# State-space stage: the step-size chain ahead of a weight split, the dense transposes in the other PSUM ring, the norm by token tile; projection units of 512 by 512

## Chip, cores and metric

The kernel runs on one core of one Trainium2 chip. The metric is device time in microseconds of one execution; three runs are given as their median. Profiled times are those of one further execution.

## What is computed

Three transformer-like blocks run one after the other on x of 1024 tokens by 1024 channels, float32. Block 1 mixes gated linear attention with a spatial gating unit and ends in an MLP. Block 2 mixes a two-way state-space scan with differential attention. Block 3 mixes a convolution branch with a gated recurrence. Each mixer ends in an output projection that is added to the residual. The part of block 2 around the change:

```
z, xbc, dt_f, dt_b, q, k, v, g = split(h @ w_in)
xbc = silu(depthwise_conv5(xbc) + b)          # 1536 channels: x, B, C
dt  = softplus(dt + dt_bias)                  # 16 heads, two directions
a_cs = cumsum(dt * A, within 128-token chunks)
y = ssd_chunked(x, dt, A, B, C), forward and backward, + D * x
y_ssm = rms_norm(y * silu(z)) per group of 512, * ssm_norm_g
mix = concat(y_ssm, y_attn) @ w_out;  h = layer_norm(ALPHA * h + mix)
```

Blocks 1 and 3 project likewise: x + concat(a, b) @ w_out, the inner dimension being 1024 in block 1 and 2048 in blocks 2 and 3, there in two parts of 1024.

## The kernel before

Every large product is made in three passes of rounded float32 (fp32r): both operands are split into a high and a low part, and high x high, high x low and low x high are summed in PSUM. `three` lists the pairs, `mms` issues them (the matmul is L211). Activations lie transposed in `HTh` and `HTl`: 8 k-tiles of 128 channels by 1024 tokens.

*Weight units.* A weight is streamed in units of 128 x 2048 elements. `sp_unit` issues the load of unit i into ring `WR` once unit i-3 has been used; `act_unit` makes the high part in `WH` (L320, after the landing and the use of unit i-2); `dve_unit` the low part in `WL` (L328, after the high part); `pe_unit` waits for both. A unit was 256 columns by 8 k-tiles. The engines' programs are written out by hand, each runs in its own order, and each unit call stands at a place chosen in that order.

*Projections.* `tm` fills one PSUM bank of 512 columns with two token tiles by 256 columns: 2 x 8 x 3 matmuls of 256 columns, the stationary operand being a tile of `HTh` or `HTl`. `dve_added` adds the bank to the residual X. `pe_proj` does four units; `pe_proj_led` two units and then two more in the order `LED`, in which the first tokens are finished early so that the next norm can start. The tags are 1 (output projection of block 1, input `sgu`), `o2a` and `o2b` (the two halves of block 2's), `o3b` and `o3c` (block 3's). `fm` is the other orientation: 24 matmuls of 512 columns into one bank.

*PSUM.* Two rings of four banks: `PD` and `PB`. `take` gives the next bank and waits for whoever must free the previous content.

*State-space stage.* `pe_ssm_first` makes the step sizes dt and the first halves of channel tiles 8 and 10. Then `weave` interleaves two generators on each engine by weights: `steps_` (the dt chain, weight 10) and `dense(0)` (channel tiles 8, 10, 0 and 1, weight 32). A channel tile m takes: fm(m,0) and fm(m,1) on TensorE; two copies into the one buffer `pad2` (L2399, ScalarE, after the convolution of the tile before) and the first tap (L2405); four more taps on VectorE (L2457); silu (L2414); transposes xbcT(m) on TensorE into `PB` (for tile 10 the CB products); copies out of them (L2378, L2383). The dt chain: transposes of dt (L2194), bias (L2261), Abs, Exp and Ln on ScalarE, softplus and dA (L2265 to L2270), the cumulative sums by matmul (ACS), their copy and differences and the row tables QT (L2275 to L2295), transposes of QT ("rows"), copies TT and LT (L2250, L2252), tables RR (L2303). Worked out from `weave`, the orders before are:

```
TensorE: dt transposes; fm 8,1; ACS; fm 10,1; rows; fm 0,0; xbcT 8 (two banks);
         fm 0,1; fm 1,0; CB (two); fm 1,1; xbcT 0; then fm 2,0; fm 2,1; xbcT 1; scan 0
ScalarE: unit; pad 8; tap; Abs,Exp,Aexp; Ln; silu 8; ldt; pad 10; tap; xs 8,0;
         exponentials; xs 8,1; TT,LT; silu 10; unit; pad 0; tap; CB; silu 0; pad 1 ...
VectorE: unit; dtb2; tap 8; dtsp,ldm,dA; taps 8; acs_; wd0,nn,QT; wd; taps 10 (two);
         RR; taps 10; unit; taps 0; diag; taps 1
```

After it four scans (`*_ssm_scan`, one for each quarter of the heads) are woven with the dense work of the next quarter. A scan step takes banks of `PB` for two segment matmuls and the states st, which L2644 adds and frees, and of `PD` for the Y and off products. After scans 1 and 3 `out_` normalises y: squares on ScalarE, two multiplies of 128 x 2048 (L2752), transposes, scaled copies (L2740) and stores.

## Time and profile before

| what | value |
|---|---|
| median of three runs | 3786.94 us (3786.23 to 3787.26) |
| the profiled execution | 3784.53 us, its span 3782.8 us |
| TensorE matmul busy | 3609.8 us, 95% of the span |
| weight loads of TensorE | 3036.7 us, 80% |
| VectorE, ScalarE, GpSimd busy | 2251.6 us, 1668.6 us, 468.9 us |
| mean granted TensorE clock | 0.98 of 2.4 GHz |

The state-space stage lies between about 1187 and 1600 us of the span; the projections at 360 to 455 (block 1), 2305 to 2470 (block 2) and 3462 to 3645 us (block 3). Busy shares are of the whole span; a group in brackets at the end of a row, `[9.33 <-DVE t L2270]`, is the time that the engine stood idle before it and the line that ended the wait.

### The profile page before, as it was taken

How to read it: one execution, taken by the hardware profiler on the slowest of the kernel's cores; microseconds unless marked ns; L12 is line 12 of the kernel's file. 1: busy time of each engine (PE TensorE's matmuls, PEld its weight loads, DVE VectorE, ACT ScalarE, POOL GpSimd, SP SyncE). 2: the span in 40 equal slices, each digit the busy share in tenths (PEclk: the TensorE clock that was granted, in tenths of full speed). 3: DMA queues.
4: the chain of work that ended last, by engine and by line, in shares of the span. 5: the costliest groups of instructions: out<-in, count | busy, mean ns of one | idle time of the engine just before them, and what ended most of it. 6: DMA issues, size and time to landing. Idle time of an engine off the chain costs nothing.

```text
span 3782.8 us, 48362 instructions
## 1 busy us (share of the span) xinstructions
PE 3609.8 (95%) x20222; PEld 3036.7 (80%) x20222; DVE 2251.6 (60%) x2947; ACT 1668.6 (44%) x2123; POOL 468.9 (12%) x373
## 2 busy tenths in 40 slices
PE   8999989999998999999999989999999999999998
PEld 7778968888876787877777759978777888778998
DVE  4545353456666765655656662468889888843332
ACT  4333344431114544467667772145455554442132
POOL 0001032200000121200000000012222222210001
PEclk9999999999999899999999999999999999999999
DMA  3012023342212011011111123121111111153111
GB/s 110 23 40 90 26 81 109 112 159 89 89 69 90 23 34 40 18 51 34 37 28 34 29 86 140 42 82 34 45 45 39 56 51 45 34 213 110 45 40 67
DMA packets 227389, 244.85 MB, mean 65 GB/s; under 512 B 10007, under 2 KB 190180, under 8 KB 227172
## 3 DMA queue, kind: packets, MB, share of 16 engines
q1 hardware_dynamic: 222391, 224.92, 18.4%
q10 hardware_dynamic: 4781, 16.84, 1.2%
q8 instruction: 160, 2.62, 0.3%
q14 instruction: 57, 0.47, 0.0%
HBM read 191.40 MB, written 50.33 MB: 64 GB/s over the span
## 4 chain that ended last, share of the span: by engine, by line
PE 77%; DVE 12%; ACT 5%; issue 3%; DMA 1%; POOL 0%; SPq 0%; ACTq 0%; DVEq 0%; POOLq 0%
PE pd L211 63%; PE pq L211 11%; PE pd L366 2%; DVE t L3520 2%; DVE t L328 1%; DVE t L3528 1%; PE pq L366 1%; DVE t L3965 1%; ACT t L3125 1%; ACT t L320 1%; DVE t L3952 0%; DVE t L3950 0%; DVE t L3197 0%; DVE t L2078 0%; DVE t L3215 0%
## 5 line engine op out<-in xcount | busy, mean ns | idle before, releaser
L211 PE MATMUL pd<-t 128*128 128x512 f32 (+2 forms) x15104 | 2904.1, 353 | 32.5 <-ACT t L3716 9.8
L211 PEld LDWEIGHTS pd<-t 128*128 128x128 f32 x15104 | 2407.6, 191 | 459.8 <-issue 90.9
L211 PE MATMUL pq<-t 128*128 128x128 f32 (+5 forms) x3782 | 635.7, 330 | 75.0 <-DVE t L4001 15.7
L211 PEld LDWEIGHTS pq<-t 128*128 128x128 f32 (+2 forms) x3782 | 484.3, 181 | 187.4 <-issue 44.4
L320 ACT ACTIVATE t<-t 128x2048 fp32r<-128x2048 f32 (+3 forms) x133 | 212.6, 1599 | 633.2 <-PE pd L211 590.8
L328 DVE TENSOR_TENSOR t<-t 128x2048 fp32r<-128x2048 f32 (+3 forms) x133 | 257.3, 1935 | 173.7 <-ACT t L320 173.2
L1919 DVE TENSOR_TENSOR t<-pd,t 128x512 f32<-128x512 f32 x256 | 172.9, 689 | 104.9 <-PE pd L211 102.7
L3248 DVE COPY t<-pd 128x512 f32<-128x512 f32 x64 | 44.2, 691 | 218.6 <-PE pd L366 218.6
L3528 DVE SCALAR_TENSOR_TENSOR t<-t 128x1024 f32<-128x1024 f32 x120 | 173.8, 1448 | 0.5
L3520 DVE SCALAR_TENSOR_TENSOR t<-t 128x1024 f32<-128x1024 f32 x120 | 169.1, 1409 | 2.1
L3917 POOL TENSOR_TENSOR t<-t 128x512 f32<-128x512 f32 x56 | 96.0, 1714 | 592.8 <-ACT t L3861 299.4
L2061 POOL TENSOR_TENSOR t<-t 128x2 f32<-128x2 f32 x8 | 10.4, 1306 | 1258.4 <-DVE t L3365 849.0
L3861 ACT ACTIVATE t<-t 128x1024 f32<-128x1024 f32 x56 | 59.5, 1062 | 228.8 <-DVE t L3952 228.8
L3125 ACT ACTIVATE t<-t 128x1024 f32<-128x1024 f32 x128 | 145.9, 1142 | 13.8 <-DVE t L3202 13.7
L3197 DVE CUSTOM_DVE_ANT_0 t<-pq,t 128x1024 f32<-128x1024 f32 x128 | 151.2, 1219 | 0.0
L366 PE MATMUL pd<-t 128*128 128x128 f32 x808 | 115.8, 285 | 25.0 <-ACT t L3106 5.9
L744 DVE TENSOR_TENSOR t<-pd,t 128x512 f32<-128x512 f32 x48 | 33.2, 691 | 175.9 <-PE pd L211 175.9
L366 PEld LDWEIGHTS pd<-t 128*128 128x128 f32 x808 | 97.4, 147 | 47.5 <-ACT t L3167 9.0
L3965 DVE COPY_PREDICATED t<-t,pq 128x512 f32<-128x512 int32 x128 | 94.4, 741 | 51.3 <-PE pq L211 50.7
L3131 ACT ACTIVATE t<-t 128x1024 f32<-128x1024 f32 x64 | 73.7, 1151 | 104.5 <-DVE t L3207 104.5
L3919 POOL TENSOR_TENSOR t<-t 128x512 f32<-128x512 f32 x56 | 112.2, 2003 | 0.0
L366 PE MATMUL pq<-t 128*128 128x128 f32 x516 | 73.7, 285 | 18.7 <-DVE t L624 5.1
(345 smaller groups left out, 2830.8 us busy)
## 6 DMA issues: line engine op xcount, KB each, us to landing
t<-in_w_in_dram SPq DMA_DIRECT2D x97, 512.0 KB, 4.3
t<-in_w_out_dram SPq DMA_DIRECT2D x20, 1024.0 KB, 5.4
t<-in_w_in_dram SPq DMA_DIRECT2D x16, 1024.0 KB, 5.3
t<-in_w_mlp_dram SPq DMA_DIRECT2D x64, 256.0 KB, 3.5
u_scratch<-t SPq DMA_DIRECT2D x64, 256.0 KB, 3.3
t<-in_w_mlp_dram SPq DMA_DIRECT2D x16, 1024.0 KB, 5.0
t<-u_scratch SPq DMA_DIRECT2D x15, 1024.0 KB, 7.2
t<-in_x_dram SPq DMA_DIRECT2D x16, 512.0 KB, 9.2
```

The lines of the kernel that those rows point to most:

```text
L211: ins = e.matmul(out, l, r, start=(first and j == 0), stop=(last and j == n - 1), skip_group_check=True)
L320: e.activation(WH[i % 2][:, 0:z], WR[i % 3][:, 0:z], ACT.Copy).then_inc(*at.inc("wh", "wh", i))
L328: e.tensor_tensor(WL[i % 3][:, 0:z], WR[i % 3][:, 0:z], WH[i % 2][:, 0:z].bitcast(F32), SUB).then_inc(*at.inc("wl", "wl", i))
L366: ins = e.transpose(b[:, j * 128:(j + 1) * 128], s, ident[:, :])
L1919: e.tensor_tensor(X1[:, tt, half(nh)], PD.of("down", j, tt, nh)[:, :], X1[:, tt, half(nh)], ADD).then_inc(*at.inc("dve", "xadd", j, tt, nh ...
L3125: e.activation(s[:, r, :], s[:, r, :], ACT.Exp, bias=x[:, 2 + r:3 + r], accum_out=x[:, 4 + r:5 + r]).then_inc(*at.inc("act", "sexp", n))
L3197: e.tensor_tensor_reduce(out=s[:, r, :], in0=PQt[r][:, :], in1=bias[:, 896 - 128 * tt:896 - 128 * tt + 1024], scale=2.0 ** -(h + 1), scala ...
L3520: e.scalar_tensor_tensor(a[:, :], p[:, k:k + S], taps(k, g), a[:, :], MUL, ADD).then_inc(*at.inc("dve", "ctaps", g))
L3528: e.scalar_tensor_tensor(a[:, :], p[:, k:k + S], taps(k, g), a[:, :], MUL, ADD).then_inc(*at.inc("dve", "ctaps", g))
L3917: e.tensor_tensor(v4(z[:, :], w_)[:, :, 0, :], v4(k[:, :], w_)[:, :, 0, :], v4(dd[:, :], w_)[:, :, 0, :], MUL).then_inc(*at.inc("pool", "h ...
L3919: e.tensor_tensor(v4(z[:, :], w_)[:, :, 1, :], v4(q[:, :], w_)[:, :, 1, :], v4(dd[:, :], w_)[:, :, 1, :], MUL).then_inc(*at.inc("pool", "h ...
L3965: e.copy_predicated(At[:, th * 4:th * 4 + 4, :], bc(Mi[:, l:l + 1, :], [128, 4, 128]), four(PB.of("lv", h, l, th))).then_inc(*at.inc("dve" ...
```

## The change

In the state-space stage, the dt chain on ScalarE and VectorE stands ahead of the weight split instead of being woven behind it, and its later parts are spaced anew (weight 16); the load of that split's weight is issued between the two halves of the stores before the stage; xbcT and CB take banks of `PD` instead of `PB`; the norm multiplies by token tile. In the projections, twelve units are 512 columns by 4 k-tiles (`pe_quarter`, one bank for each token tile, two units adding to the same columns); the `LED` units and unit 0 and 1 of `o2a` stay as they are. The orders with the new code:

```
TensorE: as before; xbcT 8, CB, xbcT 0 and all later ones now take PD
ScalarE: Abs,Exp,Aexp; Ln; ldt; unit; pad 8; tap; silu 8; pad 10; tap; xs 8 (two);
         exponentials; silu 10; unit; pad 0; tap; CB (two); TT,LT; silu 0; pad 1 ...
VectorE: dtb2; dtsp,ldm,dA; unit; taps 8; acs_; wd0,nn,QT; taps 10; unit; wd;
         tap 0 (one); RR; taps 0 (three); diag; taps 1
```

```diff
@@ -494,9 +494,9 @@
-    def sp_store_x(e, X, dst, ready, *event):
+    def sp_store_x(e, X, dst, ready, *event, tts=range(NT)):
         v = dst.rearrange("(t p) d -> p t d", p=128)
-        for tt in range(NT):
+        for tt in tts:
             e.wait_ge(*at[ready(tt)])
@@ -646,7 +646,7 @@
-        return lambda th: ("proj", tag, 3, 2 * th + 1)
+        return lambda th: ("proj", tag, 3, 4 * th + 3)
@@ -656,12 +656,31 @@
-    def pe_proj(e, W, kg, v, tag, n0=0):
-        for n in range(n0, 4):
-            u = pe_unit(e, W, [(n * 256, 256)], k0=kg * 8)
-            for t4 in range(4):
-                tm(e, u, 0, 256, [2 * t4, 2 * t4 + 1], v, "proj", tag, n, t4)
-            pe_done(u)
+    def pe_quarter(e, W, kg, kq, nh, v, tag, n):
+        u = pe_unit(e, W, [(nh * 512, 512)], k0=kg * 8 + kq * 4, k=4)
+        for tt in range(NT):
+            b = e.take(PD, "proj", tag, n, tt)
+            for k in range(4):
+                e.wait_ge(*at["HTh", v, kq * 4 + k, tt // 4])
+                e.wait_ge(*at["HTl", v, kq * 4 + k, tt // 4])
+                ins = mms(e, b[:, :], three(HTh[:, kq * 4 + k, tile(tt)], HTl[:, kq * 4 + k, tile(tt)],
+                                            u.h[:, k, :], u.l[:, k, :]), first=k == 0, last=k == 3)
+            ins.then_inc(*at.inc("pe", "proj", tag, n, tt))
+        pe_done(u)
+
+    def dve_quarter(e, X, nh, tag, n, t4, ready, alpha=None):
+        for tt in (2 * t4, 2 * t4 + 1):
+            o = X[:, tt, half(nh)]
+            b = PD.of("proj", tag, n, tt)
+            e.wait_ge(*at["proj", tag, n, tt])
+            e.wait_ge(*at[ready(tt)])
+            if alpha is None:
+                ins = e.tensor_tensor(o, b[:, :], o, ADD)
+            else:
+                ins = e.scalar_tensor_tensor(o, o, alpha, b[:, :], MUL, ADD)
+            ins.then_inc(*at.inc("dve", "added", tag, n, t4, free=("proj", tag, n, tt)))
+
+    QUARTERS = [(0, 0), (0, 1), (1, 0), (1, 1)]
@@ -669,11 +688,8 @@
     def pe_proj_led(e, W, kg, v, tag, turned_first=None):
-        for n in range(2):
-            u = pe_unit(e, W, [(n * 256, 256)], k0=kg * 8)
-            for t4 in range(4):
-                tm(e, u, 0, 256, [2 * t4, 2 * t4 + 1], v, "proj", tag, n, t4)
-            pe_done(u)
+        for kq in range(2):
+            pe_quarter(e, W, kg, kq, 0, v, tag, kq)
         us = {}
@@ -703,10 +719,10 @@
-        for n in range(2):
+        for kq in range(2):
             dve_unit(e)
             for t4 in range(4):
-                dve_added(e, X, tag, n, t4, ready0)
+                dve_quarter(e, X, 0, tag, kq, t4, lambda tt: ("added", tag, 0, tt // 2) if kq else ready0(tt))
         dve_unit(e)
@@ -1379,11 +1386,8 @@
         W = A["w_out"][0]
-        for n in range(2):
-            u = pe_unit(e, W, [(n * 256, 256)])
-            for t4 in range(4):
-                tm(e, u, 0, 256, [2 * t4, 2 * t4 + 1], "sgu", "proj", 1, n, t4)
-            pe_done(u)
+        for kq in range(2):
+            pe_quarter(e, W, 0, kq, 0, "sgu", 1, kq)
         us = {}
@@ -2044,7 +2048,9 @@
         sp_unit(e)
-        sp_store_x(e, X1, XD, lambda tt: ("emb", tt), "xd1")
+        sp_store_x(e, X1, XD, lambda tt: ("emb", tt), "xd1", tts=range(4))
+        sp_unit(e)
+        sp_store_x(e, X1, XD, lambda tt: ("emb", tt), "xd1", tts=range(4, NT))
@@ -2187,7 +2193,6 @@
     def pe_ssm_steps(e):
-        yield
         b = e.take(PB, "dt", hold=True)
@@ -2195,8 +2200,7 @@
         PB.drop("dt")
-        yield
-        yield
+        yield from idle(3)
         b = e.take(PB, "acs", hold=True)
@@ -2204,7 +2208,7 @@
         mms(e, b[:, 256:512], [(ones[:, :], flat(dA))]).then_inc(*at.inc("pe", "acs"))
-        yield
+        yield from idle(4)
         PB.drop("acs")
@@ -2218,7 +2222,6 @@
         Acc.drop("dtT")
-        yield
         e.wait_ge(*at["dtb2"])
         e.activation(Ar[:, :], Ar[:, :], ACT.Exp).then_inc(*at.inc("act", "Aexp"))
-        yield
         e.wait_ge(*at["dtexp"])
         e.activation(flat(wd), flat(wd), ACT.Ln, bias=1.0).then_inc(*at.inc("act", "dtln"))
-        yield
         e.wait_ge(*at["ldm"])
         e.activation(flat(nn), flat(nn), ACT.Ln).then_inc(*at.inc("act", "ldt"))
-        yield
+        yield from idle(8)
         b = PB.of("acs")
@@ -2242,7 +2243,7 @@
         e.activation(ea[:, ::-1, 16:32], acs[:, :, 16:32], ACT.Exp).then_inc(*at.inc("act", "ea"))
-        yield
+        yield from idle(3)
         e.wait_ge(*at["KC"])
@@ -2254,13 +2255,11 @@
     def dve_ssm_steps(e):
-        yield
         for i in range(2):
                         bc(dbr[:, :].unsqueeze(1), [128, 8, 32]), ADD).then_inc(*at.inc("dve", "dtb2", free=("dt",)))
-        yield
         e.wait_ge(*at["dtln"])
                                MUL, MUL).then_inc(*at.inc("dve", "dA"))
-        yield
+        yield from idle(6)
         b = PB.of("acs")
         e.tensor_copy(acs[:, :, :], b[:, 0:256].rearrange("p (a b) -> p a b", a=8)).then_inc(*at.inc("dve", "acs_"))
-        yield
         e.wait_ge(*at["acs_"])
@@ -2294,9 +2292,10 @@
                                 place[:, :, :, d, c, 0, :].bitcast(F32), SUB).then_inc(*at.inc("dve", "QT"))
+        yield from idle(3)
         e.wait_ge(*at["wd1"])
         e.tensor_tensor(flat(wd), flat(wd), flat(dt_), MUL).then_inc(*at.inc("dve", "wd"))
-        yield
+        yield from idle(2)
         for th in range(2):
@@ -2319,7 +2318,7 @@
             elif m < 10:
-                b = e.take(PB, "xbcT", m, th)
+                b = e.take(PD, "xbcT", m, th)
                 e.wait_ge(*at["silu", m])
@@ -2375,12 +2374,12 @@
                 e.wait_ge(*at["xbcT", m, th])
-                e.copy(o, four(PB.of("xbcT", m, th))).then_inc(*at.inc("act", "xs", m, th, free=("xbcT", m, th)))
+                e.copy(o, four(PD.of("xbcT", m, th)[:, :])).then_inc(*at.inc("act", "xs", m, th, free=("xbcT", m, th)))
                 if m < 8 and th == 1:
@@ -2747,10 +2746,9 @@
         e.wait_ge(*at["yrstd", g])
-        for p in range(2):
-            v = y[:, :, 256 * p:256 * p + 256]
-            e.tensor_tensor(v, v, bc(st[:, 0:8].unsqueeze(2), [128, 8, 256]), MUL).then_inc(
-                *at.inc("dve", "yn", g, p))
+        for tt in range(NT):
+            e.tensor_scalar(y[:, tt, :], y[:, tt, :], st[:, tt:tt + 1], None, MUL).then_inc(
+                *at.inc("dve", "yn", g, tt))
         if g == 1:
@@ -2764,8 +2762,8 @@
         for m in range(4):
-            e.wait_ge(*at["yn", g, m // 2])
             for th in range(2):
+                e.wait_ge(*at["yn", g, 4 * th + 3])
                 b = e.take(PB, "yT", g, m, th)
@@ -2792,7 +2790,7 @@
         next(first)
-        weave((first, 10), (dense(e, 0), 32))
+        weave((first, 16), (dense(e, 0), 32))
         side = ssm_side(e, 0, gate, dense, end)
         def steps_(e):
-            sp_unit(e)
             yield from idle(4)
@@ -3340,7 +3337,19 @@
-        dve_proj(e, X2, "o2a", lambda tt: ("x2", tt), ALPHA, begun=2, ahead=lambda e: load_b(e, 0))
+        for t4 in (2, 3):
+            dve_added(e, X2, "o2a", 0, t4, lambda tt: ("x2", tt), ALPHA)
+        dve_unit(e)
+        for t4 in range(4):
+            dve_added(e, X2, "o2a", 1, t4, lambda tt: ("x2", tt), ALPHA)
+        dve_unit(e)
+        for t4 in range(4):
+            dve_quarter(e, X2, 1, "o2a", 2, t4, lambda tt: ("x2", tt), ALPHA)
+        dve_unit(e)
+        for t4 in range(4):
+            if t4 == 2:
+                load_b(e, 0)
+            dve_quarter(e, X2, 1, "o2a", 3, t4, lambda tt: ("added", "o2a", 2, tt // 2))
         load_b(e, 1)
@@ -3376,7 +3388,11 @@
             for p in range(4):
-                added(n, p)
+                dve_quarter(e, X2, 0, "o2b", n, p, lambda tt: ("added", *(("o2b", 0) if n else ("o2a", 3)), tt // 2))
+                if n == 1:
+                    e.wait_ge(*at["added", "o2b", 1, p])
+                    stats(0, p)
+                    stats(1, p)
         dve_unit(e)
@@ -4231,7 +4252,12 @@
                     *at.inc("dve", "Pl", k, th, free=("pT", k, th)))
-        dve_proj(e, X3, "o3b", lambda tt: ("x3", tt), ahead=lambda e: load_c(e, 0))
+        for n, (kq, nh) in enumerate(QUARTERS):
+            dve_unit(e)
+            for t4 in range(4):
+                if (n, t4) == (3, 2):
+                    load_c(e, 0)
+                dve_quarter(e, X3, nh, "o3b", n, t4, lambda tt: ("added", "o3b", n - 2, tt // 2) if kq else ("x3", tt))
         load_c(e, 1)
@@ -4248,7 +4274,8 @@
                 transposed(e, b, [pin[:, th * 4 + j, tile(k)] for j in range(4)]).then_inc(*at.inc("pe", "pT", k, th))
-        pe_proj(e, A["w_out_3"][0], 0, "o3b", "o3b")
+        for n, (kq, nh) in enumerate(QUARTERS):
+            pe_quarter(e, A["w_out_3"][0], 0, kq, nh, "o3b", "o3b", n)
         pe_squares(4, 0)
...
```

## Rows read from the trace of the kernel before

**Rows 1.** The page, part 4: shares of the chain that ended last.
```profile
PE 77%; DVE 12%; ACT 5%; issue 3%; DMA 1%; POOL 0%; SPq 0%; ACTq 0%; DVEq 0%; POOLq 0%
```

**Rows 2.** Windows: length, busy us (x) of PE, PEld, DVE, ACT, POOL; clock, DMA, GB/s.
```profile
3403.00:3426.00 23.00, 23.00 (x103) 19.04 (x102) 8.07 (x7) 3.83 (x2) 0.00 (x0) 1.00 0.49 155
...
3486.00:3509.00 23.00, 23.00 (x194) 23.00 (x194) 5.02 (x6) 1.88 (x2) 0.00 (x0) 1.00 0.15 47
```

**Rows 3.** Chain in order of time: start, us, what.
```profile
3462.60 178.56 PE pd L211 x1488
```

**Rows 4.** Timeline of TensorE, 1193 to 1262: start, us, engine, line, tiles.
```profile
1193.21 0.43 PE L2194 MATMUL pq<-t 32*128 32x32 f32 x4 [0.30 <-ACT t L2219]
...
1208.67 2.05 PE L211 MATMUL pq<-t 128*128 128x128 f32 x6 [9.33 <-DVE t L2270]
...
1210.15 7.99 PE L211 MATMUL pd<-t 128*128 128x512 f32 x24
...
1227.77 12.75 PE L211 MATMUL pd<-t 128*128 128x512 f32 x48
...
1248.30 1.09 PE L366 MATMUL pq<-t 128*128 128x128 f32 x8 [0.51 <-ACT t L2414]
...
1249.15 11.16 PE L211 MATMUL pd<-t 128*128 128x512 f32 x48
```

**Rows 5.** Timeline of ScalarE and VectorE, same stretch.
```profile
1198.74 1.91 ACT L320 ACTIVATE t<-t 128x2048 fp32r<-128x2048 f32 x1 [5.58 <-DMA t<-in_w_in_dram]
...
1200.75 2.29 DVE L328 TENSOR_TENSOR t<-t 128x2048 fp32r<-128x2048 f32 x1 [10.95 <-ACT t L320]
...
1202.96 0.42 DVE L2261 TENSOR_TENSOR t<-pq,t 128x256 f32<-128x256 f32 x1
...
1208.10 0.42 DVE L2270 SCALAR_TENSOR_TENSOR t<-t 128x256 f32<-128x256 f32 x1
...
1225.56 1.28 ACT L2239 ACT_TABLE_LOAD   x1
...
1229.01 1.46 ACT L2252 ACTIVATE t<-pq,t 128x512 fp32r<-128x512 f32 x2
...
1231.06 2.98 DVE L2303 TENSOR_SCALAR t<-t 128x1024 fp32r<-128x1024 f32 x4 [0.48 <-ACT t L2250]
...
1236.71 1.06 ACT L2414 ACTIVATE t<-t 128x1024 f32<-128x1024 f32 x1 [3.12 <-DVE t L2457]
...
1240.63 1.24 ACT L2405 ACTIVATE t<-t 128x1024 f32<-128x1024 f32 x1
...
1241.91 5.25 DVE L2457 SCALAR_TENSOR_TENSOR t<-t 128x1024 f32<-128x1024 f32 x4
```

**Rows 6.** Waits of TensorE, 1262 to 1450: us in total, times, longest.
```profile
PE pq L211 <- DVE t L2644: 7.8, 3, 3.2
```

**Rows 7.** Timeline of VectorE: evictions of groups of 24 512-column matmuls.
```profile
3428.25 0.75 DVE L4225 SCALAR_TENSOR_TENSOR t<-pd,t 128x512 f32<-128x512 f32 x1 [4.62 <-PE pd L211]
...
3433.76 0.75 DVE L4225 SCALAR_TENSOR_TENSOR t<-pd,t 128x512 f32<-128x512 f32 x1 [4.76 <-PE pd L211]
...
3439.13 0.75 DVE L4225 SCALAR_TENSOR_TENSOR t<-pd,t 128x512 f32<-128x512 f32 x1 [4.62 <-PE pd L211]
```

**Rows 8.** The same in the down projection: groups of six.
```profile
906.97 0.69 DVE L1919 TENSOR_TENSOR t<-pd,t 128x512 f32<-128x512 f32 x1 [0.71 <-PE pd L211]
908.37 0.69 DVE L1919 TENSOR_TENSOR t<-pd,t 128x512 f32<-128x512 f32 x1 [0.71 <-PE pd L211]
909.73 0.69 DVE L1919 TENSOR_TENSOR t<-pd,t 128x512 f32<-128x512 f32 x1 [0.67 <-PE pd L211]
```

**Rows 9.** The same view, one stretch of the first scan.
```profile
1299.00:1306.00 7.00, 7.00 (x24) 5.25 (x24) 6.76 (x10) 2.50 (x3) 2.16 (x2) 0.58 0.01 2
```

**Rows 10.** Timeline of the norm, and the form of another tensor_scalar.
```profile
1450.45 5.31 DVE L2752 TENSOR_TENSOR t<-t 128x2048 f32<-128x2048 f32 x2 [1.75 <-POOL t L2760]
...
L1448 DVE TENSOR_SCALAR t<-t x8: 747/748/754, 437.2 to 467.8; 128x1024 f32<-128x1024 f32 x8
```

More of the change, by code:

```diff
@@ L726, in dve_norm_led @@
             dve_split_k(e, k, v, 1, gname)
-    def dve_proj(e, X, tag, ready, alpha=None, begun=0, ahead=lambda e: None):
-        for n in range(4):
-            if not (begun and n == 0):
-                dve_unit(e)
-            for t4 in range(begun if n == 0 else 0, 4):
-                if (n, t4) == (3, 2):
-                    ahead(e)
-                dve_added(e, X, tag, n, t4, ready, alpha)
     def dve_added(e, X, tag, n, t4, ready, alpha=None):
@@ L1452, in loaded_x @@
             return "x1", tt
-        for n in range(2):
+        for kq in range(2):
             dve_unit(e)
             for t4 in range(4):
-                dve_added(e, X1, 1, n, t4, loaded_x)
+                dve_quarter(e, X1, 0, 1, kq, t4, lambda tt: ("added", 1, 0, tt // 2) if kq else loaded_x(tt))
         dve_unit(e)
@@ L2331, in pe_ssm_late @@
                 e.wait_ge(*at["silu", m])
-                b = e.take(PB, "cb", m - 10, th)
+                b = e.take(PD, "cb", m - 10, th)
                 for j in range(4):
@@ L2382, in act_ssm_late @@
                 e.wait_ge(*at["cb", i // 2, th])
-                e.copy(CB[:, th * 4:th * 4 + 4, :], four(PB.of("cb", i // 2, th))).then_inc(
+                e.copy(CB[:, th * 4:th * 4 + 4, :], four(PD.of("cb", i // 2, th)[:, :])).then_inc(
                     *at.inc("act", "CB", i // 2, th, free=("cb", i // 2, th)))
@@ L3409, in pe_out2 @@
     def pe_out2(e):
-        pe_proj(e, A["w_out_2"][0], 0, "o2a", "o2a", n0=1)
+        u = pe_unit(e, A["w_out_2"][0], [(256, 256)])
+        for t4 in range(4):
+            tm(e, u, 0, 256, [2 * t4, 2 * t4 + 1], "o2a", "proj", "o2a", 1, t4)
+        pe_done(u)
+        for kq in range(2):
+            pe_quarter(e, A["w_out_2"][0], 0, kq, 1, "o2a", "o2a", 2 + kq)
         pe_proj_led(e, A["w_out_2"][0], 1, "o2b", "o2b")
@@ L4233, in dve_out3 @@
                     *at.inc("dve", "Pl", k, th, free=("pT", k, th)))
[L4234 removed]
+        for n, (kq, nh) in enumerate(QUARTERS):
+            dve_unit(e)
+            for t4 in range(4):
+                if (n, t4) == (3, 2):
+                    load_c(e, 0)
+                dve_quarter(e, X3, nh, "o3b", n, t4, lambda tt: ("added", "o3b", n - 2, tt // 2) if kq else ("x3", tt))
         load_c(e, 1)
```

2 lines of the change are left out of this document (added).

## The prediction

> **What bounds the kernel now.** I read the chain of waits first. [rows 1] is its share by engine: three quarters of the chain that ended last is the matmul engine, and one line of code (L211, the three-product matmul helper) carries almost all of it. So the question for every edit is what it does to TensorE's own time and to TensorE's waits; work on the other engines counts only where TensorE waits for it. I then took the two places that the diff touches.
>
> *Projection stretches.* [rows 2] sets two 23 us windows side by side: one with 256-column matmuls (a projection), one with 512-column matmuls. TensorE is busy throughout both. The weight-load row is what differs: 23.00 of 23 us in the first, 19.04 in the second. The 256-wide stretch is paced by weight loads, one for each matmul. [rows 3] gives that pace from the chain: 1488 matmuls in 178.56 us, 120.0 ns each. VectorE is free there most of the time.
>
> *Start of the state-space stage.* [rows 4] is TensorE's timeline. It stands 9.33 us before the cumulative-sum matmuls (ACS), and the 24 matmuls after it take 7.99 us. In [rows 5] the reason is visible from left to right: ScalarE's weight split (L320) waited 5.58 us for a DMA, VectorE's split (L328) follows it, and only then comes the first step-size operation L2261, whose input was ready at 1193.7 [rows 4]. Its last, L2270, ends at 1208.5. Later in this stage TensorE waits for L2644, an addition that frees a bank of the `PB` ring [rows 6].
>
> **Projection units.** A unit of 256 columns by 8 k-tiles is 4 x 2 x 8 x 3 = 192 matmuls: 192 x 120.0 ns = 23.04 us [rows 3]. The new quarter, 512 columns by 4 k-tiles, is 8 x 4 x 3 = 96 matmuls of 512 columns. Twelve units change: two for output projection 1 (`sgu`), two of `o2a`, two of `o2b`, four of `o3b`, two of `o3c`; the reordered `LED` halves stay 256 wide. The trace has no 512-wide projection, so I bound it by the two nearest rows. Full-k groups of 24 such matmuls are evicted 5.51 and 5.37 us apart, mean 5.44 [rows 7]: 96/24 x 5.44 = 21.76 us. In the down projection, whose stationary operand is an activation tile as in the new unit, groups of six come every 1.40 or 1.36 us [rows 8]: 96/6 gives 22.4 or 21.76 us. So a unit saves 0.64 to 1.28 us; I take 1.1, between the mean of the down pace (0.96) and the full-k pace: 12 x 1.1 = **13.2 us** (7.7 to 15.4).
>
> What could eat it: each quarter is evicted in eight adds of 0.69 us [rows 8] rather than four, 2.8 us more VectorE work per unit, and a bank now fills in 12 x 0.227 = 2.7 us instead of 5.76. Four banks are 10.9 us. The longest time VectorE is away is a stage change: last eviction 0.7, eight low-part loads of a 512-column tile (eight times 0.69 at most, 5.5), weight split 2.29 [rows 5], then the first eviction, 0.7: 9.2 us. That is under 10.9, so I cost it at nothing; beyond it every us would be TensorE's, at four such places. The second accumulation into the same columns needs the first one's add, 22 us earlier: nothing. Weight splits keep their size. `proj_read` frees the input halves at the same halves of the last unit. Four statistics of 256 columns for each pair of tiles now stand together in the second unit of `o2b`, each under the 0.69 of an add, so under 2.8 us beside two adds in a slot of 5.4 us: hidden.
>
> The Trainium skill ("TensorE: Matmul & The Clock Gate", Back-to-back issue gap) gives an isolated gap of N/2.4 + 2.5 ns. By it 192 x 109.2 = 20.96 us becomes 96 x 215.8 = 20.72, a saving of 0.24 us a unit, 2.9 us over twelve, instead of 13.2, and a sum of -5.3 instead of -15.6. The trace's 120.0 ns at 256 columns speaks against it, and so does the full weight-load share beside it.
>
> **State-space start.** I wrote out the order that `weave` gives with the new counts. The DMA of the first x unit is now issued ahead of the last four stores (one unit call moved past SP's queue, none added; it lands in a gap of the DMA engines), so ScalarE no longer waits for it. The chain L2261 to L2270 is 5.56 us long [rows 5] and starts at 1193.7: it ends at 1199.3, just when TensorE ends its matmuls. The 9.33 us are gone. What is late next, step by step, with durations of [rows 5]:
> 1. ScalarE's split now stands behind the chain: 1199.4 to 1201.3; two pad copies (0.57 each), first tap (1.24) to 1203.6. VectorE's split to 1203.7, four taps 5.25 to 1209.0, then copy, differences and row tables: ten small operations that I take at 2.9 from their sizes (0.42 for 256 columns), to 1211.9. TensorE needs them for the rows transposes. It had begun fm(10,1) when the first pad copy freed its bank, 1202.0, and needs 5.5: a new wait from 1207.5, 4.4 us, and a low clock behind it (below).
> 2. Rows transposes 1.1, fm(0,0) 5.5, 2 of clock: 1220.7; transposes of tile 8 to 1221.8. ScalarE, which stands waiting for them, copies them (to 1222.5), loads a table (1.28), makes five exponentials (1.2), loads another, silu of tile 10 (1.06) to 1227.3, next split to 1229.1, pad copy (0,0) at 1229.65.
> 3. The transposes now take banks of `PD`, so fm(1,0) gets the bank of fm(0,0), not that of fm(8,1): it waits for this pad copy, 2.35 us. It ends near 1236.9 if the clock falls, else 1235.2; the CB products to 1238.9.
> 4. The LT/TT copies (two copies and two pairs of 1.46, 3.8; the second TT after 2.4) moved behind the CB copies: second TT at 1241.9. RR on VectorE (2.98) waits for it *between the first and second tap of tile 0*: to 1244.9, remaining taps 3.9 to 1248.8, silu and pad copy (1,0) to 1250.5.
> 5. Transposes of tile 0 take the bank of fm(1,0) and so wait for pad (1,0): 1250.5 against 1248.30 before [rows 4], after 6 us of idling. Two fm of 5.5 follow: their end, which gates the first scan through pad, tap and x copies, is 1264.6 against 1260.3 before.
>
> So in place of one wait of 9.3 there are three of 4.4, 2.35 and 6.1. The clock: in [rows 4] 24 matmuls took 7.99 after the 9.33 wait where 5.5 is usual, and 48 took 12.75 after 2.43 where 11.0 is usual; I charge 2, 1.7 and 2. If none of these falls, the start is 1.4 us earlier than before. I take 3 us later, **+3** (-1.5 to +5).
>
> **Scans.** `PB` no longer carries the transposes. The waits for L2644 are 7.8 us in three [rows 6]. Written out, st(0,5) waited for the bank of st(0,4); now it gets an earlier one, and the next segment matmul waits for the same add 2 us later: 1 us instead of 2.98, and with it perhaps the 0.58 clock of 7 us [rows 9], up to 2.9. The wait of 1.58 keeps 1, that of 3.24 goes. Against it, transposes and Y products in `PD` now wait for pad copies of the next tile, which stand one ScalarE step behind the silu they wait for anyway: 0.3 us each, 1.5 in all. Net **-5** (-9 to +1).
>
> **Norm by token tile.** Two 2.65 us multiplies [rows 10] become eight of 512 columns. A tensor_scalar of 1024 columns is 0.748 [rows 10]; I take 0.42 for 512, between its half, 0.37, and a quarter of a multiply, 0.66. Eight are 3.4. The first product tile's first half can be turned after four, 1.7 instead of 2.65; its second half, which its store needs, after eight, 3.4, where before the first half's turning and copy (1.2) lay in between. Group 0 gains about 0.4, and in group 1 TensorE has 512-wide matmuls to do meanwhile: **-0.4** (-2 to +1.5).
>
> **Sum.** -13.2 + 3 - 5 - 0.4 = -15.6 us. The profiled execution took 3784.53 us (span 3782.8), so 3768.9 there; the median shown is 2.4 above it: 3786.94 - 15.6 = 3771.3.
>
> **Rivals.** (a) *The step-size chain's time is kept*: the clock stays up, the pad and RR waits are smaller, and start and scans give -12 together: 3786.9 - 13.2 - 12 = 3762. For it: 9.33 us vanish for sure. Against: steps 3 to 5. Chance 0.13. (b) *Width buys nothing*: a 512-wide matmul with an activation tile as stationary costs two 256-wide ones, 240 ns, since the two low-part products force the same waits; then 3786.9 - 2.4 = 3784.5. For it: no row shows just this form. Against: [rows 2], [rows 8]. Chance 0.06. The page's gap rule would leave a fifth of the gain. (c) *The start gives back most*: +4.3, scans keep nothing (+1.5): 3786.9 - 13.2 + 5.8 = 3779.5. Chance 0.14. (d) *Slower: `PD` as the bottleneck.* If each of the eleven channel tiles behind the first makes TensorE wait 2.4 us for a pad copy and pay 1.7 of clock, that is 45 us in place of the state-space terms: 3786.9 - 13.6 + 45 = 3818. It decides from 13.6/11 = 1.2 us a tile. Against: in the written order most pad copies are done before the bank comes round. Chance 0.05. The forecast itself (-6 to -22, 3765 to 3781) has 0.62.
>
> A difference of 0.2% (7.6 us) is about what can be told from none. Faster: 0.59 of the forecast, (a), half of (c): 0.79. Slower: (d), 0.05. Within: the forecast's edge 0.03, (b), half of (c): 0.16. The range takes in (a) and most of (c): 3761 to 3782.
>
> **What would show it.** In the trace after: 96 matmuls of 512 columns in 21.8 to 22.4 us in the projections, no wait for the adds there; no wait of 9 us before ACS; new waits of TensorE for VectorE's row tables, for pad copies (L2399) and before the tile 0 transposes; the first segment matmul of the scan, at 1261.1 before, between 1260 and 1265; L2644 gone from the longest waits. Wrong would be: evictions that hold TensorE in projections, or a scan start earlier than 1257.

## The result, and the profile after

The changed kernel takes 3777.17 us in the median of 7 runs (3771.07 to 3779.20); before took 3787.01 beside it (3785.76 to 3791.73). That is 9.8 us less, ratio 0.9970, 95% interval 0.9958 to 0.9981. A second series of the same kernel gave 15.8 us less (ratio 0.9957, 0.9944 to 0.9971; e5 below). In microseconds the two intervals are 7 to 16 and 11 to 21. The forecast was 15.6 us less and 3771.3, with a range of 6 to 22 us less.

The page, part 4, shares of the chain that ended last [rows 1]:

```profile
PE 79%; DVE 10%; ACT 6%; issue 3%; DMA 1%; POOL 0%; ACTq 0%; DVEq 0%; SPq 0%; POOLq 0%
```

*Projections.* The window and the chain (start, us, what) that answer to [rows 2, 3]:

```profile
3486.00:3509.00 23.00, 23.00 (x103) 19.06 (x102) 8.52 (x10) 2.27 (x2) 0.00 (x0) 1.00 0.18 62
```

```profile
352.41 88.98 PE pd L211 x528
...
3462.55 170.91 PE pd L211 x912
```

The window now looks like the 512-column one of before: 19.06 us of weight loads instead of 23.00. The last stretch of matmuls holds the same work in 170.91 instead of 178.56 us: 576 matmuls fewer are six units, 7.65 us, 1.275 a unit. Block 1's is 88.98 against 91.54 (two units, 1.28 each). Block 2's, on the timeline, is 156.40 against 161.50 (four, 1.275 each). Together 15.3 us, and no eviction holds TensorE inside any of them: the chain and the timeline have each stretch as one row without an idle time in it.

*Start of the state-space stage.* TensorE's timeline, for [rows 4]:

```profile
1193.12 0.43 PE L2199 MATMUL pq<-t 32*128 32x32 f32 x4
...
1200.15 1.12 PE L211 MATMUL pq<-t 128*128 128x128 f32 x6 [0.19 <-DVE t L2269]
1202.45 5.73 PE L211 MATMUL pd<-t 128*128 128x512 f32 x24 [1.18 <-ACT t L2398]
1211.98 1.97 PE L366 MATMUL pq<-t 128*128 128x128 f32 x8 [3.80 <-DVE t L2293]
1213.60 7.70 PE L211 MATMUL pd<-t 128*128 128x512 f32 x24
...
1230.01 14.63 PE L211 MATMUL pd<-t 128*128 128x512 f32 x64 [2.35 <-ACT t L2398]
1250.76 1.97 PE L366 MATMUL pd<-t 128*128 128x128 f32 x8 [6.12 <-ACT t L2398]
1252.38 12.54 PE L211 MATMUL pd<-t 128*128 128x512 f32 x48
...
1265.72 0.73 PE L211 MATMUL pq<-t 32*128 32x512 f32 x4
```

ScalarE and VectorE in the same stretch, for [rows 5]:

```profile
1229.39 1.06 ACT L2398 COPY t<-pd 128x512 f32<-128x512 f32 x2
...
1241.48 0.60 ACT L2251 COPY t<-pq 128x512 f32<-128x512 f32 x1
...
1242.19 2.98 DVE L2302 TENSOR_SCALAR t<-t 128x1024 fp32r<-128x1024 f32 x4 [8.78 <-ACT t L2251]
1245.21 3.92 DVE L2456 SCALAR_TENSOR_TENSOR t<-t 128x1024 f32<-128x1024 f32 x3
```

The 9.33 us ahead of ACS are 0.19. Read upward from the 6.12: TensorE waits for a pad copy (L2398) that follows silu 0, which follows the taps (L2456), which stand behind RR (L2302), which waited 8.78 us for the second TT copy (L2251). The last row of TensorE is the scan's first segment matmul. From the dt transposes (1193.12) to it I count 72.60 us; before it was 1192.48 to 1261.11, 68.63. This distance is free of what happens earlier in the kernel, and I use it from here on, as "the start". It is not free of noise: kernels with the same code in this stage lie up to 1.5 us apart (72.60, 72.52 and 71.06 for after, e5 and e2).

*Scans.* TensorE's waits from 1266 to 1450 (us in total, times, longest), for [rows 6], and two windows, the second for [rows 9]:

```profile
PE pq L211 <- POOL t L2578: 4.7, 2, 2.8
PE pq L211 <- DVE t L2643: 1.8, 2, 1.6
PE pd L366 <- DVE t L2617: 1.0, 1, 1.0
PE pd L211 <- DVE t L2652: 0.7, 1, 0.7
...
```

Before has for GpSimd, in its view from 1262 to 1450:

```profile
PE pq L211 <- POOL t L2579: 2.9, 2, 1.9
```

```profile
1279.70:1293.70 14.00, 14.00 (x54) 10.97 (x53) 9.30 (x14) 5.43 (x6) 6.30 (x8) 0.77 0.00 1
...
1303.70:1310.70 7.00, 4.68 (x26) 3.66 (x24) 6.79 (x10) 2.39 (x3) 2.09 (x2) 1.00 0.03 11
```

The add that frees PB banks holds TensorE 1.8 us instead of 7.8. Against that, waits for PD banks of 1.0 and 0.7 us are new, and the waits for GpSimd are 1.8 us longer. In the second window the clock is 1.00 where it was 0.58, but TensorE is busy for only 4.68 of 7.00 us, so that nearly the same number of matmuls runs in it (26, before 24). The first window, which follows a longer idle stretch, runs at 0.77.

*Norm.* TensorE and VectorE, for [rows 10]:

```profile
1447.53 0.17 DVE L2747 TENSOR_SCALAR t<-t 128x8 f32<-128x8 f32 x1 [5.03 <-ACT t L2727]
...
1449.45 3.95 DVE L2750 TENSOR_SCALAR t<-t 128x512 f32<-128x512 f32 x8 [1.75 <-POOL t L2758]
1451.88 0.65 PE L366 MATMUL pq<-t 128*128 128x128 f32 x4 [1.75 <-DVE t L2750]
1453.46 3.98 PE L366 MATMUL pq<-t 128*128 128x128 f32 x20 [0.93 <-DVE t L2750]
...
1462.67 1.24 PE L211 MATMUL pq<-t 128*128 128x256 f32 x4 [2.72 <-ACT t L2739]
```

VectorE needs 3.95 us instead of 5.31, but TensorE's product tiles wait twice, and from the mean squares (first row) to the next scan's first matmul (last row) it is 15.14 us, where before had 1448.53 to 1462.88, 14.35.

The median has not shown the 15.3 us of the projections at once. Single executions of one kernel lie up to 9 us apart (before: 3783.68 to 3792.45 in 18 runs), so two medians of 7 can differ by some us without a cause. That was the question for the first runs: do the parts add up?

### The profile page after: what moved, and what is told of

The parts are those of the page before. It is cut to its first block, busy times and chain, and to the rows that moved or that the text cites. A ratio compares the mean times of both kernels' runs of the same rounds, so it can differ in the third digit from the quotient of the medians.

```text
span 3775.1 us, 46097 instructions
## 1 busy us (share of the span) xinstructions
PE 3596.8 (95%) x19070; PEld 2977.3 (79%) x19070; DVE 2277.2 (60%) x3007; ACT 1669.5 (44%) x2122; POOL 464.2 (12%) x373
## 4 chain that ended last, share of the span: by engine, by line
PE 79%; DVE 10%; ACT 6%; issue 3%; DMA 1%; POOL 0%; ACTq 0%; DVEq 0%; SPq 0%; POOLq 0%
PE pd L211 65%; PE pq L211 12%; PE pd L366 2%; DVE t L328 1%; DVE t L3541 1%; PE pq L366 1%; DVE t L3549 1%; ACT t L3122 1%; ACT t L320 1%; DVE t L3986 1%; DVE t L2456 0%; DMA yc_scratch<-t 0%; DVE t L3971 0%; DMA ym_scratch<-t 0%; DVE t L2084 0%
## 5 line engine op out<-in xcount | busy, mean ns | idle before, releaser
L211 PEld LDWEIGHTS pd<-t 128*128 128x128 f32 x13984 | 2349.6, 191 | 513.4 <-issue 93.2
L1923 DVE TENSOR_TENSOR t<-pd,t 128x512 f32<-128x512 f32 x256 | 172.8, 689 | 103.3 <-PE pd L211 101.2
L3549 DVE SCALAR_TENSOR_TENSOR t<-t 128x1024 f32<-128x1024 f32 x120 | 173.1, 1443 | 0.5
L3541 DVE SCALAR_TENSOR_TENSOR t<-t 128x1024 f32<-128x1024 f32 x120 | 170.4, 1420 | 2.1
L366 PE MATMUL pd<-t 128*128 128x128 f32 x888 | 127.6, 285 | 35.3 <-ACT t L2398 6.1
L366 PEld LDWEIGHTS pd<-t 128*128 128x128 f32 x888 | 106.3, 146 | 59.9 <-ACT t L3164 9.5
L678 DVE TENSOR_TENSOR t<-pd,t 128x512 f32<-128x512 f32 x88 | 59.8, 690 | 108.5 <-PE pd L211 108.5
L3212 DVE SCALAR_TENSOR_TENSOR t<-t 128x1024 f32<-128x1024 f32 x64 | 81.9, 1279 | 0.3
```

Of the source, the lines that this page charges most:

```text
L211: ins = e.matmul(out, l, r, start=(first and j == 0), stop=(last and j == n - 1), skip_group_check=True)
L366: ins = e.transpose(b[:, j * 128:(j + 1) * 128], s, ident[:, :])
L1923: e.tensor_tensor(X1[:, tt, half(nh)], PD.of("down", j, tt, nh)[:, :], X1[:, tt, half(nh)], ADD).then_inc(*at.inc("dve", "xadd", j, tt, nh ...
L3541: e.scalar_tensor_tensor(a[:, :], p[:, k:k + S], taps(k, g), a[:, :], MUL, ADD).then_inc(*at.inc("dve", "ctaps", g))
L3549: e.scalar_tensor_tensor(a[:, :], p[:, k:k + S], taps(k, g), a[:, :], MUL, ADD).then_inc(*at.inc("dve", "ctaps", g))
```

## Experiments

| run | kernel | median us (runs) | ratio to before, 95% | start |
|---|---|---|---|---|
| after | the changed kernel | 3777.17 (7) | 0.9970, 0.9958 to 0.9981 | 72.60 |
| e1 | projection units alone | 3775.28 (8) | 0.9971, 0.9961 to 0.9981 | 67.84 |
| e2 | state-space part alone | 3787.28 (11) | 0.9997, 0.9988 to 1.0006 | 71.06 |
| e3 | early tables, first tiles in PB | 3760.87 (5) | 0.9931, 0.9919 to 0.9944 | 59.82 |
| e4 | row tables earlier still | 3763.74 (5) | 0.9936, 0.9923 to 0.9950 | 61.47 |
| e5 | the changed kernel again | 3772.64 (5) | 0.9957, 0.9944 to 0.9971 | 72.52 |
| e6 | PD banks alone | 3787.44 (1) | | 75.53 |
| e7 | first tiles in PB, order kept | 3767.09 (1) | | 69.81 |
| e8 | early tables, all in PD | 3767.36 (1) | | 65.42 |
| e9 | e3 with the old norm | 3759.53 (5) | 0.9926, 0.9914 to 0.9939 | 58.73 |
| e10 | e3 again | 3759.54 (5) | 0.9928, 0.9914 to 0.9941 | 58.67 |
| e11, e12 | e1 with 256-column matmuls | 3787.81 (10), 3788.26 (10) | 1.0001, 0.9996 | |

Before had medians of 3787.01, 3788.55 (beside e1 to e4), 3788.40 (e5 to e8), 3787.64 (e9, e10), 3787.71 (e11) and 3789.98 (e12). "Start" is the distance defined above; before has 68.63.

e6, e7 and e8 are single executions. Their times can't be told from one another within some us, and what is read from them below are distances in their profiles.

**The two parts apart: e1 and e2.** e1 is the kernel before with every hunk that touches `pe_quarter`, `dve_quarter` and their calls; e2 takes all the other hunks of the diff.

> The kernel before with the twelve projection units alone. Theory: each unit gains what the trace after shows, 15.3 us over twelve (2.55 + 5.1 + 7.65), and it reaches the end: 15 us faster than before, ratio 0.996. Rival 1: the wide units cost something later (the mix stage of block 3, which lost 4 us in the one profile of after): 11 us faster and the mix stage 4 us longer than before in this profile too. Rival 2: my rows were flattered and it gains 10 or less with no place of loss. The time over which 1488 matmuls of 256 columns stood should show 171 to 172 us instead of 178.6.

> The kernel before with the state-space part alone: step-size chain first, transposes and CB in the other ring, norm by token tile. Theory from the trace after: start +4, scans -5, norm and output +0.8, so 0 (-1 to +1) against before. Rival: if the whole kernel gained 9.8 where the projections gained 15.3, the state-space part and what follows it cost about 5: +5. In the profile: waits of TensorE of about 3.8, 2.35 and 6.1 us at the start, first segment matmul 4 us later than before.

e1 gained 13.3 us, e2 1.3. By the intervals e1 gains 7 to 15 us, and e2 lies between 5 us gained and 2 lost. So both theories are possible, the 5 us lost of e2's rival are not; the medians alone don't decide between e1's theory (15) and its first rival (11). The rows do for the units themselves. In e1's chain of waits the last stretch is

```profile
3468.70 170.91 PE pd L211 x912
```

the same 170.91 as in the changed kernel.

**Again the whole: e5.**

> The changed kernel once more, against before. Its 9.8 us rest on seven runs whose times lie up to 8 us apart. If the two parts add up (13.3 of the projections alone, 1.3 of the state-space part alone), it is 14.6 us faster, ratio 0.9961; if they disturb one another, it stays at 9.8, ratio 0.9974. In its profile the wait ahead of the first product of block 3's last block should again be 3.8 to 4.2 us instead of 2.4, as in every kernel so far with the wide units.

It gained 15.8 us, and the parts (14.6) lie inside both series' intervals: nothing shows that their meeting costs. The twelve executions of the changed kernel together have a median of 3776.1 against 3788.1 for the sixteen of before beside them, about 12 us less. That the first 9.8 was low by chance is possible and not shown.

The second guess of this run was wrong in its cause. It rested on the stretch between the projections of blocks 2 and 3, which has the same code in all kernels. From the last matmul of the one to the first of the other it takes 996.0 us before and 999.9 after. e2, without wide units, has 998.0 there and e6, also without, 1001.5, with the "wide-unit" wait at 3.63 us in it. So the wait comes without wide units too, and before's 996.0 is the shortest of all. A small effect of the change isn't excluded: the nine profiles with wide units have 998.3 to 1001.9, 1000.4 in the mean, the five with 256-column matmuls 996.0 to 1001.5, 998.5 in the mean. That would be 2 us of the 15.3.

**What the three waits hang on: e3, e6, e7, e8.** e6 is before with the change of banks alone. e7 and e8 undo one half each of what e3 undoes together. The core of e3 (e8 is its second part alone, e7 its first without CB, and with the exponentials put between the copies of tile 8):

```diff
+    def turned(m):
+        return PB if m in (8, 10, 0, 1) else PD
-                b = e.take(PD, "xbcT", m, th)
+                b = e.take(turned(m), "xbcT", m, th)
...
-        weave((first, 16), (dense(e, 0), 32))
+        weave((first, 15), (dense(e, 0), 32))
...
         e.activation(flat(nn), flat(nn), ACT.Ln).then_inc(*at.inc("act", "ldt"))
-        yield from idle(8)
+        yield from idle(5)
...
         e.activation(ea[:, ::-1, 16:32], acs[:, :, 16:32], ACT.Exp).then_inc(*at.inc("act", "ea"))
-        yield from idle(3)
+        yield from idle(2)
...
-        yield from idle(3)
+        yield from idle(2)
         e.wait_ge(*at["wd1"])
         e.tensor_tensor(flat(wd), flat(wd), flat(dt_), MUL).then_inc(*at.inc("dve", "wd"))
-        yield from idle(2)
+        yield from idle(0)
```

ScalarE then runs tap 10, exponentials, copies of tile 8, TT and LT, silu 10; VectorE runs wd and RR ahead of its weight split.

> The changed kernel with the first four channel tiles' transposes and CB back in PB (later ones stay in PD), and with the exponentials, TT and LT on ScalarE ahead of the silu of tile 10 and RR ahead of the weight split on VectorE. If the 2.35 us wait comes from the PD bank of fm(0,0) and the 6.1 us one from RR standing between the taps of tile 0, both go (a wait of up to 2.1 for the silu of tile 0 stays): the first segment matmul comes at 1255 to 1258 instead of 1265.7, and the kernel is 7 to 9 us faster than the changed one, 17 to 19 faster than before. Rival: the silu of tile 10 comes 4 us later behind TT and LT, CB waits for it, and the 6.1 us only move there: 1263 or later, at most 2 us gained.

> The kernel before with the turned tiles and CB in PD, and nothing else. Counted from the transposes of dt, the first segment matmul stood at 68.6 us before and 72.6 after. In the old order the pad copy (0,0) comes at 1240, so the second product of tile 1 waits 6.6 us for the bank of fm(0,0): 74 to 75 us. Rival: the wait comes from the new order on ScalarE alone, then 68 to 69. In the scans the waits for the addition that frees PB banks fall from 7.8 to about 2 us and the scans end 5 us sooner, whichever is right at the start.

> The changed kernel with the transposes of tiles 8, 0 and 1 back in PB (CB stays in PD, TT and LT stay behind the CB copies; the exponentials stand between the two copies of tile 8). If the 2.35 us wait is that of a PD bank, it goes, and what hangs on it moves 2 to 5 us ahead: first segment matmul at 68 us from the transposes of dt (72.6 in the changed kernel, 59.8 in the kernel with everything in PB and the early order). The wait before the transposes of tile 0 stays (5 to 8 us), its releaser is then silu of tile 0 (L2416) instead of the pad copy. Rival: the banks matter little, all is the order: 71 or later.

> The changed kernel with exponentials, TT, LT and RR early as in e3, all banks as in the changed kernel. If RR between the taps of tile 0 made the 6.1 us wait, it goes, while the wait for the pad copy (0,0) stays and grows, as TT and LT now stand ahead of it: 3 to 4 us; first segment matmul at 64.5 us (63 to 66) from the transposes of dt. Rival: with PD banks the wait before the transposes of tile 0 stays at 4 or more, 68 or later.

TensorE's timeline of e3:

```profile
1210.50 1.97 PE L366 MATMUL pq<-t 128*128 128x128 f32 x8 [3.75 <-DVE t L2293]
...
1220.43 11.16 PE L211 MATMUL pd<-t 128*128 128x512 f32 x48
1231.43 1.95 PE L211 MATMUL pq<-t 128*128 128x128 f32 x16
1233.13 5.74 PE L211 MATMUL pd<-t 128*128 128x512 f32 x24
1238.71 1.03 PE L366 MATMUL pq<-t 128*128 128x128 f32 x8
1239.51 11.16 PE L211 MATMUL pd<-t 128*128 128x512 f32 x48
```

Of the three waits only the first is left; from 1220 to the first segment matmul TensorE doesn't stand, and 48 matmuls take 11.16 us instead of 12.54. The same timeline of e6, e7 and e8:

```profile
1208.35 2.05 PE L211 MATMUL pq<-t 128*128 128x128 f32 x6 [10.86 <-DVE t L2270]
...
1238.87 14.71 PE L211 MATMUL pd<-t 128*128 128x512 f32 x64 [9.11 <-ACT t L2399]
```

```profile
1219.92 0.66 PE L366 MATMUL pq<-t 128*128 128x128 f32 x4 [2.43 <-ACT t L2241]
1220.33 18.46 PE L211 MATMUL pd<-t 128*128 128x512 f32 x88
1244.52 1.94 PE L366 MATMUL pq<-t 128*128 128x128 f32 x8 [5.73 <-ACT t L2416]
```

```profile
1209.19 1.80 PE L366 MATMUL pq<-t 128*128 128x128 f32 x8 [3.79 <-DVE t L2293]
...
1227.33 15.84 PE L211 MATMUL pd<-t 128*128 128x512 f32 x64 [3.58 <-ACT t L2398]
1243.01 1.03 PE L366 MATMUL pd<-t 128*128 128x128 f32 x8
```

e6: with PD banks and the old order the wait for the pad copy is 9.11 us (forecast 6.6: before's wait of 2.43 us ahead of the tile 8 transposes is gone with the PB bank, and TensorE comes to this one sooner) and the start 75.53 (forecast 74 to 75), 6.9 later than before. In its scans the waits for the freeing add are 1.8 us, and from the first segment matmul to the first mean squares it takes 178.83 us against 187.42 before. So PD pays in the scans and costs at the start, and alone it nets out (3787.44 against 3788.40, one execution). e7: the 2.35 us wait is gone with the bank, the last one stays at 5.73 and names silu 0 as forecast; the start is 69.81 and not 68, since TensorE now waits 2.43 us for the exponential that frees a PB bank, which I had not priced. e8: the wait before the transposes of tile 0 is gone, the pad wait has grown to 3.58, start 65.42 (forecast 64.5). So banks and order are separate causes: the order costs 7.1 us (72.5 - 65.4), the banks 5.6 more with the early order in place (65.4 - 59.8; 6.8 against e10's 58.7). Both cures together give 12.8 us at the start and 27 to 28 us against before, e3 and e10 alike. I had forecast 7 to 9 less than the changed kernel for e3 and a first segment matmul at 1255 to 1258; it stands at 1251.47. I had left a wait of 2.1 us and its clock loss in the sum that did not occur.

**Row tables earlier: e4.** As e3, with everything of the chain a step earlier: on VectorE the row tables ahead of the taps of tile 8 (the line shown) and RR behind them, on ScalarE exponentials, TT and LT ahead of silu 8.

```diff
                                MUL, MUL).then_inc(*at.inc("dve", "dA"))
-        yield from idle(6)
+        yield from idle(2)
```

> As the kernel before this one in the list, and the row tables of VectorE stand ahead of the taps of tile 8, the exponentials, TT and LT ahead of the silu of tile 8, RR between the taps of 8 and 10. If the 3.8 us wait ahead of the rows transposes comes from the taps that stand ahead of the row tables, it goes too and every later chain starts some 5 us sooner: first segment matmul at 1246 to 1250, 16 to 20 us less than in the changed kernel; the kernel 24 to 29 us faster than before if the scans keep what they have. Rival: the taps of tile 8 come 3 us later, so silu and pad copy of the next tile do, and TensorE waits for a PD bank instead: 1253 or later.

TensorE's timeline of e4:

```profile
1204.95 1.04 PE L366 MATMUL pq<-t 128*128 128x128 f32 x8
1212.33 7.49 PE L211 MATMUL pd<-t 128*128 128x512 f32 x24 [6.34 <-ACT t L2401]
```

VectorE and ScalarE ahead of that pad copy (L2401):

```profile
1203.55 5.24 DVE L2459 SCALAR_TENSOR_TENSOR t<-t 128x1024 f32<-128x1024 f32 x4
...
1207.87 1.48 ACT L2253 ACTIVATE t<-pq,t 128x512 fp32r<-128x512 f32 x2
1209.36 1.28 ACT L2416 ACT_TABLE_LOAD   x1
1210.65 1.06 ACT L2416 ACTIVATE t<-t 128x1024 f32<-128x1024 f32 x1
```

My theory fell, and the rival held in its effect: the rows transposes come without a wait, and the next matmuls wait 6.34 us for the pad copy of tile 10 instead. That copy follows silu of tile 8 (L2416). The rival had put its delay down to the taps, and they are only part of it. Counted from the dt transposes, silu 8 begins at 20.6 us, in e3 at 16.4. The taps (L2459) end 2.4 us later than in e3, behind the row tables; the other 1.9 us are ScalarE's own, which is still busy with TT, LT and a table load when the taps are done. So a second wait stood behind the 3.8 us one, and removing the one that the row named uncovered the other, a little later: start 61.47 against 59.82 (58.67 in the repetition, e10). The kernel is 24.8 us faster than before, inside the 24 to 29 of the theory, but only since e3 without this step had 27.7.

**Norm: e9 and e10.** e9 is e3 with the two multiplies of 128 x 2048 and the wait of each product tile for its half.

> The kernel of e3 with the norm's two multiplies of 128 x 2048 as before. I had put the change of the norm at -0.4. In the traces, from the mean squares (the 128 x 8 operation on VectorE) to the first matmul of the next scan it is 14.35 us before, 15.14 with the norm by token tile: the second half of the first product tile now waits for all eight operations, 3.95 us. Theory: the old form gives 14.0 to 14.4 there, and the kernel is 0 to 1.5 us faster than e3 on the same chip. Rival: the order of the multiplies doesn't matter, since the later product tiles wait for their stores anyway: 15.1 stays.

> The kernel of e3 again, as the measure for e9 on the same chip: 26 to 29 us faster than before, 14.8 to 15.4 us from the mean squares to the first matmul of the next scan.

Mean squares, TensorE's first transposes and the next scan's first matmul, e9 and then e10:

```profile
1428.99 0.17 DVE L2750 TENSOR_SCALAR t<-t 128x8 f32<-128x8 f32 x1 [5.01 <-ACT t L2730]
...
1433.66 4.51 PE L366 MATMUL pq<-t 128*128 128x128 f32 x24 [2.05 <-DVE t L2754]
...
1443.03 2.08 PE L211 MATMUL pq<-t 128*128 128x256 f32 x4 [2.72 <-ACT t L2742]
```

```profile
1427.23 0.17 DVE L2750 TENSOR_SCALAR t<-t 128x8 f32<-128x8 f32 x1 [5.01 <-ACT t L2730]
...
1433.16 3.81 PE L366 MATMUL pq<-t 128*128 128x128 f32 x20 [0.93 <-DVE t L2753]
...
1442.39 1.58 PE L211 MATMUL pq<-t 128*128 128x256 f32 x4 [2.71 <-ACT t L2742]
```

14.04 against 15.16 us: the old form is 1.1 us shorter here, as forecast. But its matmuls behind (2.08 us for four instead of 1.58) run at a lower clock: 0.50 in the 4 us from there, against 0.57. At the wait for GpSimd in the next scan (3.36 us in both) 90.11 and 90.30 us have passed since the mean squares, and the medians are 3759.53 and 3759.54. The norm's form decides nothing.

**Width or shape: e11 and e12.** Both are e1 with each 512-column matmul issued as two of 256. In e11 the two interleave k-tile by k-tile in one bank, and the projections no longer give the right sums, so that e11 counts only for the time of its matmuls; in e12 the first 256 columns come whole before the second, and it computes what e1 does. Banks, loads and adds are those of the wide units.

```diff
-            for k in range(4):
...
-                ins = mms(e, b[:, :], three(HTh[:, kq * 4 + k, tile(tt)], HTl[:, kq * 4 + k, tile(tt)],
-                                            u.h[:, k, :], u.l[:, k, :]), first=k == 0, last=k == 3)
+            for c in (slice(0, 256), slice(256, 512)):
+                for k in range(4):
...
+                    ins = mms(e, b[:, c], three(HTh[:, kq * 4 + k, tile(tt)], HTl[:, kq * 4 + k, tile(tt)],
+                                                u.h[:, k, c], u.l[:, k, c]), first=k == 0, last=k == 3)
```

> The kernel of e1 (projection units alone) with each matmul of 512 columns issued as two of 256 into the halves of the same bank; unit shape, banks, adds and their order stay as in the wide units. Theory: what gains is the width of a matmul, as 256 columns are paced by the weight load at 120.0 ns; then the units take 23.04 us again, the projection of block 3 has its 178.8 us back from 171.15, and the kernel is within 3 us of before. Rival: the unit shape gains (eight banks to a unit, two waits for input tiles less for each), then 171 to 173 us stay, and 10 us or more against before.

> As e11, but all of a bank's first 256 columns ahead of its second 256, so that the two sums don't interleave. The order within a bank is another, the matmuls, banks, loads and adds are the same. Theory as before: the matmul width alone is what gains, 178.6 us for the 1488 matmuls of block 3's stretch, within 3 us of before. Rival: the interleaved order hid a gain of the unit shape; then 175 or less, 5 us or more faster than before.

Chain and window of e12:

```profile
3466.52 178.56 PE pd L211 x1488
```

```profile
3486.00:3509.00 23.00, 23.00 (x194) 23.00 (x193) 7.73 (x9) 1.92 (x1) 0.00 (x0) 1.00 0.13 46
```

The 178.56 us are back to the hundredth and the weight loads fill the window again; e11 has 178.56 as well. The gain of the units is the width of a matmul and not their shape. Each matmul of these kernels has its own weight load, so no run tells the width apart from half as many weight loads, and none tries two 256-column matmuls behind one load.

## Why the prediction was right, point by point

*Projection units*, forecast -13.2, bounds 7.7 to 15.4: in the rows -15.3 (e1's median, -13.3, can't say it that finely). The mechanism held (e12) and the term was mis-sized: I took 1.1 us a unit between the down projection's pace and the full-k one, and it was 1.275, the 21.76 us of the full-k rows [rows 7]. The down projection's slower groups (1.40 us, [rows 8]) did not come back in the new units; no run shows what makes them slower.

By the gap rule of the Trainium skill ("TensorE: Matmul & The Clock Gate", Back-to-back issue gap), N/2.4 + 2.5 ns, a unit would have gained 0.24 us by estimate; 1.275 were measured. Neither of its figures agrees here: the 256-column matmuls take 120.0 ns and not 109.2, the 512-column ones 226.7 and not 215.8.

*What could eat it*, costed at nothing: nothing did. TensorE's 156.40 us of block 2 stand without a break through four stage changes of VectorE.

*Start of the stage*, forecast +3 with all three waits, +4.3 in its full form: measured +3.97, and step by step: rows transposes wait 3.80 (forecast 4.4), clock loss behind 2.0 (2; 7.70 us against 5.73), fm(1,0) behind pad copy (0,0) at 1230.0 (1229.65) after 2.35 (2.35), second TT done 1242.1 (1241.9), end of RR 1245.2 (1244.9), transposes of tile 0 at 1250.76 (1250.5) after 6.12 (6.1), clock loss 1.4 (2; 12.54 against 11.16), end of fm(2,1) 1264.9 (1264.6). No clock loss followed the 2.35 us wait, where 1.7 was charged if it came: 64 matmuls in 14.63 us. Writing out the order of each engine and laying known durations along it gave the whole stage. The first segment matmul, at 1265.72, lies 0.7 us beyond the 1260 to 1265 that I had named as its place; its stage began 0.64 us later than before. Whether 4.3 had to be shaded to 3 can't be told: against 68.63 of before, e5 gives +3.9 and e2, with the same code there, +2.4. The clock losses are the loose part: in eight kernels 24 matmuls of the same place, behind waits of 3.75 to 3.80 us, took 6.57 to 7.70 us.

*Scans*, forecast -5: from the first segment matmul to the first mean squares 187.42 us before, 181.81 after (-5.6), and from there to the second mean squares 145.00 and 146.23, of which e6 has 146.02 with the banks alone (+1.0): -4.6. The L2644 waits went from 7.8 to 1.8 as priced. The 4.6 is good to some us only: with the code of before in the second stretch e1 has 148.38 and e12 143.34, and e6, whose scans are those of the changed kernel, has 178.83 in the first.

*Norm*, forecast -0.4: +0.8 up to the next scan, +0.2 further behind (e9 against e10, and 146.23 against 146.02 above). The step that was off: the eight operations took 3.95 us, not 3.4 (0.49 each, where 0.42 was taken), and the second half of the first product tile waits for all of them.

*Sum*: -15.3 + 4.0 - 4.6 + 0.2 = -15.7, against -15.6 forecast. That it meets to 0.1 us is luck: two errors of opposite sign are in it (units 2.1 more, the rest 2.0 less). e5 measured -15.8, the first series -9.8, both together about -12, so the sum is confirmed to some us and no finer. The profiled executions don't show it either: the span is 3782.8 us before and 3775.1 in both profiles of the changed kernel, 7.7 less. The other 8.0 us of the first one lie where the code is the same, 2.9 of them ahead of block 1's projection (it begins at 349.51 and 352.41) and 3.9 between those of blocks 2 and 3. The forecast for the profiled execution, 3768.9, was therefore 8.3 too low.

*Rivals.* (b) is excluded by the rows, 170.91 against 178.56 us, and e12 says why; (d) by the waits: those for PD banks between 1266 and 1450 us are 1.0 us and less, not 2.4 a tile. (c), 3779.5, is the one that the first median, 3777.17, comes closest to. Its first half came true, the start gave back 4.0; its second didn't, since from the first segment matmul to the first mean squares the changed kernel needs 5.6 us less. (a), the chain's time kept, was not what the change did, but e3 shows that it was there to be had: 27.7 us less than before, 12.4 of them beside the 15.3 of the projections. What stood against it, steps 3 to 5, was the bank of tile 1 and the place of TT, LT and RR.
